# Another order of Strassen's seven products in the last gate of an encoder kernel

## The reference

```python
def _trunk(x, p, g_pre, g_post, w_ple, w_ple_gate, ...):
    for i in range(DEPTH):
        h = _rmsnorm(x, g_pre[i])
        ...
        x = x + _rmsnorm(o, g_post[i])
        x = x + jax.nn.sigmoid(x @ w_ple_gate[i]) * (p[i] @ w_ple[i])
    return x
```

## Time and profile before

| | us |
|---|---|
| median of three runs | 2026.52 |
| the profiled execution's own time | 2028.59 |
| its span, first to last instruction | 2026.8 |
| TensorE busy | 1929.4 |
| VectorE busy | 1174.0 |
| GpSimd busy | 781.5 |
| ScalarE busy | 689.6 |

### The profile page before, as it was taken

The page is one execution under the profiler, slowest core; times in us unless marked ns, Lnnn a source line. Parts: engine busy times, 40 slices in busy tenths (PEclk is TensorE's granted clock), DMA queues, the critical chain, the costliest instruction groups (busy, mean ns, idle before and its releaser), DMA issues. The chain is left out here.

```text
span 2026.8 us, 26398 instructions
## 1 busy us (share of the span) xinstructions
PE 1929.4 (95%) x9784; PEld 1607.2 (79%) x9784; DVE 1174.0 (58%) x1735; ACT 689.6 (34%) x1397; POOL 781.5 (39%) x552
## 2 busy tenths in 40 slices
PE   4999999999989999999999999999999999999699
PEld 3788888887889788788777888777989897887577
DVE  5599999736768227416743100365777773267675
ACT  6111212211668322112322111223777773323231
POOL 0110121122687444535433223213535362545473
PEclk9999999999989999999999999998999999999799
DMA  4202333443566646534211222583212225565424
GB/s 165 66 11 68 139 90 114 135 144 112 183 233 223 203 164 234 174 104 153 97 51 46 77 78 89 191 293 109 63 48 63 46 78 165 187 214 190 153 94 146
DMA packets 145185, 263.03 MB, mean 130 GB/s; under 512 B 30705, under 2 KB 69361, under 8 KB 144434
## 3 DMA queue, kind: packets, MB, share of 16 engines
q1 hardware_dynamic: 145074, 261.54, 39.4%
HBM read 173.22 MB, written 88.28 MB: 129 GB/s over the span
## 5 line engine op out<-in xcount | busy, mean ns | idle before, releaser
L589 DVE SCALAR_TENSOR_TENSOR ie_acc<-ie_u,ie_wconv,ie_acc 128x1551 f32<-128x1551 f32 x120 | 248.9, 2074 | 3.2
L187 POOL TENSOR_TENSOR w_lo_part<-w_raw,w_hi_part 128x1024 fp32r<-128x1024 f32 x24 | 67.3, 2804 | 333.7 <-ACT w_hi_part L179 333.7
L169 POOL TENSOR_TENSOR w_hi_part<-w_raw,zero 128x1024 fp32r<-128x1024 f32 x52 | 99.9, 1921 | 173.9 <-DMA w_raw<-wall 171.6
L1515 PE MATMUL op_ps<-w_hi_part,rows_hi 128*128 128x512 f32 x384 | 156.8, 408 | 5.1 <-DVE rows_lo L1153 2.6
L324 PE MATMUL ie_ps<-rows_hi,w_hi_part 128*128 128x512 f32 x384 | 152.4, 397 | 4.8 <-DVE w_lo_part L553 4.8
L324 PE MATMUL ie_ps<-rows_lo,w_hi_part 128*128 128x512 f32 x384 | 152.6, 397 | 0.0
L1515 PE MATMUL op_ps<-w_lo_part,rows_hi 128*128 128x512 f32 x384 | 152.2, 396 | 0.0
L1515 PE MATMUL op_ps<-w_hi_part,rows_lo 128*128 128x512 f32 x384 | 152.2, 396 | 0.0
L324 PE MATMUL ie_ps<-rows_hi,w_lo_part 128*128 128x512 f32 x384 | 150.9, 393 | 0.0
L171 POOL TENSOR_TENSOR w_lo_part<-w_raw,w_hi_part 128x1024 fp32r<-128x1024 f32 x52 | 130.1, 2503 | 4.1
L2851 DVE TENSOR_TENSOR mla_pt_lo<-mla_ps_t,mla_pt_hi 128x512 fp32r<-128x512 f32 x160 | 109.0, 686 | 26.2 <-ACT mla_pt_hi L2820 24.9
(11 more groups left out here) (289 smaller groups left out, 5184.1 us busy)
## 6 DMA issues: line engine op xcount, KB each, us to landing
w_raw<-wall SPq DMA_DIRECT2D x86, 512.0 KB, 4.8
op_in<-x SPq DMA_DIRECT2D x24, 512.0 KB, 4.5
x<-op_in SPq DMA_DIRECT2D x24, 512.0 KB, 3.0
pro_x<-x SPq DMA_DIRECT2D x12, 512.0 KB, 9.8
op_in<-attn SPq DMA_DIRECT2D x24, 256.0 KB, 2.9
o_half<-op_ost SPq DMA_DIRECT2D x24, 256.0 KB, 2.0
gt_p_raw<-p_fm SPq DMA_DIRECT2D x48, 128.0 KB, 3.3
op_orl<-o_half SPq DMA_DIRECT2D x24, 256.0 KB, 5.1
```

The lines of the kernel that those rows point to most:

```text
L169: pool.tensor_tensor(hi, raw, g.zero[:, 0:1].broadcast_to([P, QCOLS]), ALU.add).then_inc(g.w_hi, 1)
L589: dve.scalar_tensor_tensor(acc[:], ubuf[:, cc, s:s + CW], wconv[:, cc, s:s + 1], acc[:], ALU.mult, ALU.add).then_inc(taps, 1)
L1515: mm = pe.matmul(product_at(c * NT + t), g.XT[a][:, k, t * P:(t + 1) * P], w_at(g, name, m, k * HALF, HALF), start=k + a + m == 0, stop=k ...
```

## The change

The seven passes come in another order: A11, A12, S4, S2, S3, S1, A22. Output tiles are now finished in three passes: one a unit in A12, two a unit in S1, one a unit in A22; a third partial sum `Y` is held in the place of S4's rows. Three kinds of work change engine. The sums and low parts of the weights go from GpSimd to VectorE (`w_step`, 16 instructions of 1024 columns), except the sums for T1 and T4. The sum S1 of the rows goes from VectorE to GpSimd. The embeddings' high parts, from tile 2 on, go from GpSimd to ScalarE (`rows_high`); GpSimd keeps their low parts (`rows_low`). In the SyncE queue the embeddings are loaded before the residual rows, no longer after them, and only one weight block is loaded in the middle of the A12 pass, where one block and two quarters were. The diff, cut to its core:

```diff
                               self.g.XT[0][:, 2 * a:2 * a + 2, 0:HALF].bitcast(F32), ALU.subtract).then_inc(self.lo, 2)
 
 
-SEVEN = ("A11", "A12", "S2", "S3", "S1", "S4", "A22")
+SEVEN = ("A11", "A12", "S4", "S2", "S3", "S1", "A22")
...
     def sum_s2(self, dve, j):
-        dve.wait_ge(self.summed_k, 2 * j + 1)
-        dve.tensor_tensor(self.s2(j), self.row(1, 1, j), self.row(0, 0, j), ALU.subtract).then_inc(self.summed, 1)
+        dve.wait_ge(self.sums["S3"], j + 1)
+        dve.tensor_tensor(self.spare_at(j), self.row(1, 1, j), self.row(0, 0, j), ALU.subtract).then_inc(self.sums["S2"], 1)
 
     def sum_s4(self, dve, j):
         dve.wait_ge(self.lo, PAIRS_OF_TILES + j + 1)
-        dve.wait_ge(self.summed, 2 * j + 1)
-        dve.tensor_tensor(self.row(0, 1, j), self.row(0, 1, j), self.s2(j), ALU.subtract).then_inc(self.summed, 1)
+        dve.wait_ge(self.sums["S2"], j + 1)
+        dve.tensor_tensor(self.row(0, 1, j), self.row(0, 1, j), self.spare_at(j), ALU.subtract).then_inc(self.sums["S4"], 1)
+
+    def sum_s1(self, pool, j):
+        pool.wait_ge(self.sums["S3"], j + 1)
+        pool.tensor_tensor(self.row(1, 0, j), self.row(1, 0, j), self.row(1, 1, j), ALU.add).then_inc(self.sums["S1"], 1)
...
+        w_summed = {n: sem("sum_" + n) for n in ("T2", "T3", "T1", "T4")}
+        w_hi, w_lo = sem("w_hi"), sem("w_lo")
+
+        OUTPUTS = {1: [(0, 0)], 5: [(1, 1), (0, 1)], 6: [(1, 0)]}
+        UNITS = []
+        of_unit = [[] for _ in range(NU)]
+        for n in range(NU):
+            i, j = divmod(n, PAIRS_OF_TILES)
+            for half, c in OUTPUTS.get(i, []):
+                of_unit[n].append(len(UNITS))
+                UNITS.append((half * PAIRS_OF_TILES + j, c))
+        E = len(UNITS)
+        taken_by = [0]
+        for n in range(NU):
+            taken_by.append(taken_by[-1] + (n // PAIRS_OF_TILES in (2, 3, 4)))
+
+        SLOT = {"A11": (1, 0), "A12": (1, 1), "S4": (0, 0), "S2": (0, 1), "S3": (1, 0), "S1": (1, 1), "A22": (0, 0)}
+        BLOCK = {"B22": (0, 0), "T2": (0, 1), "T3": (1, 0), "T1": (1, 1), "T4": (0, 0)}
+        READY = ["B22", "T2", "T3", "T1", "T4"]
+        OF_PASS = {"S4": "B22", "S2": "T2", "S3": "T3", "S1": "T1", "A22": "T4"}
...
+            def load_embedding(e):
+                if e < 4:
+                    sp.wait_ge(ple.p_split, 2 * (e - 1))
+                else:
+                    sp.wait_ge(p_lo, e - 3)
+                sp.dma_start(ple.p_raw[:, e % 2], g.p_fm[l, UNITS[e][0]]).then_inc(ple.p_in[e % 2], 16)
...
-                    load_raw(B11, 1)
+                    load_block("T3", B22)
                 if n == 12:
...
+                for e in of_unit[n]:
+                    if e + 2 < E:
+                        load_embedding(e + 2)
+                for e in of_unit[n]:
+                    if e + 2 < E:
+                        load(e + 2)
+                    sp.wait_ge(x2_rows, 2 * (e + 1))
+                    t, c = UNITS[e]
+                    sp.dma_start(tiles_of(g.y, t)[:, c * HALF:(c + 1) * HALF], x2[:, e % 3]).then_inc(stored[e % 3], 16)
...
-            def low(name, q):
-                pool.wait_ge(w_hi, 2 * READY.index(name) + q + 1)
-                pool.tensor_tensor(quarter(name, q, 1), quarter(name, q), quarter(name, q, 0).bitcast(F32), ALU.subtract).then_inc(w_ready, 1)
...
-            ple.split_rows(pool, 2)
-            ple.split_rows(pool, 3)
-            low("T3", 0)
-            ple.split_rows(pool, 4)
-            low("T3", 1)
-            ple.split_rows(pool, 5)
+            def rows_low(e):
+                hi, lo = [x[:, e % 2] for x in ple.p]
+                pool.wait_ge(p_hi, e - 1)
+                pool.tensor_tensor(lo, ple.p_raw[:, e % 2], hi.bitcast(F32), ALU.subtract).then_inc(p_lo, 1)
+
+            for e in range(2, 6):
+                rows_low(e)
+            ple.split_weights(pool, 1)
...
+            rows_low(6)
+            rows_low(7)
+            for j in range(PAIRS_OF_TILES):
+                bl.sum_s1(pool, j)
...
-            W_HIGH = {4: ("T2", 0), 5: ("T2", 1), 6: ("T3", 0), 7: ("T3", 1), 14: ("T1", 0), 15: ("T1", 1),
-                      20: ("T4", 0), 21: ("T4", 1), 22: ("B22", 0), 23: ("B22", 1)}
+            W_HIGH = {5: ("B22", 0), 6: ("B22", 1), 11: ("T2", 0), 12: ("T2", 1), 15: ("T3", 0), 16: ("T3", 1),
+                      22: ("T1", 0), 23: ("T1", 1), 28: ("T4", 0), 29: ("T4", 1)}
...
+            def rows_high(e):
+                act.wait_ge(ple.p_in[e % 2], 16 * (e // 2 + 1))
+                act.wait_ge(ple.mm, e - 1)
+                act.copy(ple.p[0][:, e % 2], ple.p_raw[:, e % 2]).then_inc(p_hi, 1)
...
-                if whole(n) is not None:
-                    tanh(whole(n))
+                for e in of_unit[n]:
+                    tanh(e)
+                for e in of_unit[n]:
+                    if e + 2 < E:
+                        rows_high(e + 2)
...
+            W_STEPS = {6: ("T2", 0, 0), 7: ("T2", 0, 1), 8: ("T2", 1, 0), 9: ("T2", 1, 1), 10: ("B22", 2, 0), 11: ("B22", 2, 1),
+                       12: ("T3", 0, 0), 13: ("T3", 0, 1), 14: ("T2", 2, 0), 15: ("T2", 2, 1), 20: ("T3", 2, 0), 21: ("T3", 2, 1),
+                       26: ("T1", 2, 0), 27: ("T1", 2, 1), 32: ("T4", 2, 0), 33: ("T4", 2, 1)}
+
+            def w_step(name, step, q):
+                at = quarter(name, q)
+                if step == 0:
+                    dve.wait_ge(block_in[name], 16)
+                    dve.wait_ge(raw_in[q], 16)
+                    dve.tensor_tensor(at, at, g.raw[:, q], ALU.subtract).then_inc(w_summed[name], 1)
+                elif step == 1:
+                    dve.wait_ge(block_in["B22"], 16)
+                    dve.wait_ge(w_summed[name], q + 1)
+                    dve.tensor_tensor(at, at, quarter("B22", q), ALU.add).then_inc(w_summed[name], 1)
+                else:
+                    dve.wait_ge(w_hi, 2 * READY.index(name) + q + 1)
+                    if name == "T1":
+                        dve.wait_ge(w_summed["T4"], q + 1)
+                    dve.tensor_tensor(quarter(name, q, 1), at, quarter(name, q, 0).bitcast(F32), ALU.subtract).then_inc(w_lo, 1)
...
                 elif i == 5:
-                    dve.wait_ge(taken, 2 * PAIRS_OF_TILES + j + 1)
-                    total(e, u, product).then_inc(totalled, 1)
+                    dve.wait_ge(taken, taken_by[n - PAIRS_OF_TILES + 1])
+                    total(of_unit[n][0], v, product)
+                    total(of_unit[n][1], y, product)
                 else:
-                    total(e, v, product).then_inc(totalled, 1)
+                    total(of_unit[n][0], v, product)
...
             for n in range(NU + 1):
                 if n + AHEAD < NU:
                     bl.low(dve, n + AHEAD)
-                j = n - 4
                 if n < PAIRS_OF_TILES:
-                    bl.sum_k(dve, n)
-                if 0 <= j < PAIRS_OF_TILES:
-                    bl.sum_s2(dve, j)
+                    bl.sum_s3(dve, n)
+                if 0 <= n - 2 < PAIRS_OF_TILES:
+                    bl.sum_s4(dve, n - 2)
+                if n < PAIRS_OF_TILES:
+                    bl.sum_s2(dve, n)
+                if n in W_STEPS:
+                    w_step(*W_STEPS[n])
+                for e in of_unit[n - 1] if n else []:
+                    row(e)
                 if PAIRS_OF_TILES <= n < NU:
                     consume(n)
-                if 0 <= j < PAIRS_OF_TILES:
-                    bl.sum_s4(dve, j)
-                if n and whole(n - 1) is not None:
-                    row(whole(n - 1))
...
             def embedding(e):
-                c = COLS[e // PAIRS_OF_TILES]
+                c = UNITS[e][1]
                 if e == 0:
                     pe.wait_ge(bl.copied, NT)
-                pe.wait_ge(ple.p_split, 2 * (e + 1))
+                if e < 2:
+                    pe.wait_ge(ple.p_split, 2 * (e + 1))
+                else:
+                    pe.wait_ge(p_lo, e - 1)
+                    pe.wait_ge(x2_rows, 2 * (e - 2) + 1)
                 pe.wait_ge(ple.w_split, 2 * (c + 1))
-                if e >= 2:
-                    pe.wait_ge(x2_rows, 2 * (e - 2) + 1)
```

More of the change, by code:

```diff
@@ L1188, in source @@
         name = SEVEN[i]
-        return {"A11": self.row(0, 0, j), "A12": self.row(0, 1, j), "S2": self.s2(j), "S3": self.row(0, 0, j),
+        return {"A11": self.row(0, 0, j), "A12": self.row(0, 1, j), "S2": self.spare_at(j), "S3": self.row(0, 0, j),
                 "S1": self.row(1, 0, j), "S4": self.row(0, 1, j), "A22": self.row(1, 1, j)}[name]
@@ L1194, in wait_source @@
         name = SEVEN[i]
[L1195 to L1198, removed]
+        if name in self.sums:
+            eng.wait_ge(self.sums[name], j + 1)
         else:
@@ L1787, in gate_seven @@
         V = bl.spare_at
+        Y = lambda j: bl.row(0, 1, j)
         G = lambda e: bl.spare_at(PAIRS_OF_TILES + e % 2)
@@ L1793, in gate_seven @@
```

(21 more changed lines are left out.)

100 lines of the change are left out of this document (35 added, 65 removed).

## The result

The changed kernel takes 2034.25 us in the median of 7 runs (2029.59 to 2035.79); the kernel before, in 7 runs beside it, 2024.83 us (2022.59 to 2027.62). The ratio is 1.004, 95% interval 1.0028 to 1.0052: slower by some 9 us, where 1.0 was forecast. The profiled execution took 2034.25 us, its span is 2032.4, its mean granted clock 0.981.

A forecast was written before the change was run, and what follows sets the result against it. Waits in A12 through VectorE's row and GpSimd's low part bounded it beside TensorE's work. A12 gives 4.9 us, the rest costs 5.9: 1.0 more, median 2026.52 to 2027.5; range 2014 to 2037, forecast's own 2022.5 to 2032 (chance 0.50).

The forecast's parts named there:

- D: S1 pass: lower clock holds for whole units behind waits, TensorE becomes the bound; 9.2 us more, 2036.7; chance 0.10.
- E: A12 and S1 rounds meet GpSimd's low parts of embeddings, S2 and S3 fall behind; 8 more, 2035.5; chance 0.13.
- the two loads of an S1 round: S1, two tiles a unit: loads put at 2.8 us in a round of 7.9, or 9.1 with a T4 step.
- GpSimd in VectorE's way: End of A12: GpSimd's split of embeddings' weights delays the row's second instruction by 0 to 2.2 us, taken as 1.7.
- the lower clock behind A12: Lower clock counted at 1.5 us within product 12, nothing for the 17 products after it.
- Row of tile 0: Start of A12: first row instruction at 1870.8, so embedding(2) starts there and not at 1883.77; 12.9 us won.
- The round: A12 and S1: each row waits for a load the previous row set off; 7.3 us in A12 against TensorE's 4.2.
- S4, S2 and S3 without a wait: 17 products without an embedding: moved weight work costs nothing; passes at 50 us without a wait.
- S1: 43.9 forecast: S1 pass takes 43.9 us, 10.3 more than 33.6; against 4.4 lost before, the rest costs 5.9 more.
- A22 and the tail: A22: no high parts of rows left, 4.2 us a unit, loads awaited three rows later; costs nothing, tail the same.
- B: Shorter rounds: loads land 1.9 us after issue, seven rounds 0.9 shorter, no GpSimd meeting; 8 us less, 2019.5; chance 0.17.
- C: Round does not close: cast never late, only the block's load stops TensorE in A12, S1 loses nothing; 2006.6; chance 0.10.

The follow-up runs named there:

- Experiments 2: Changed kernel with ScalarE's cast of the embeddings one place later, behind the next high part of rows: 2007.28 us, ratio 0.9918 to the kernel before.
- 7: Changed kernel with the cast behind the next high part, plus the ten low parts of weights back on GpSimd: 2013.58 us, ratio 0.9945 to the kernel before.
- version 3: Changed kernel with SyncE loading tile e+4's embeddings ahead of its wait for row(e), embedding(3)'s ahead of the T3 block: 2014.07 us, ratio 0.9943.
- versions 9: Changed kernel with later cast and earlier embedding loads, plus B22's two low parts on GpSimd: 2010.41 us, ratio 0.9909 to the kernel before.
- 10: Changed kernel with later cast, earlier embedding loads and B22's low parts on GpSimd, plus ScalarE's next high part ahead of tanh: 1991.18 us, ratio 0.9828.
- 5: Changed kernel with the cast behind the next high part, plus embedding(3)'s load ahead of the T3 block: 2007.85 us, ratio 0.9923 to the kernel before.
- 6: Changed kernel with both the cast behind the next high part and embeddings loaded two tiles earlier: 2005.74 us, ratio 0.9908 to the kernel before.

## Why the prediction was wrong in size

The sign of its sum and its mechanism were right, and 2034.25 lies in the range. The forecast time was wrong: the loss is 9 us, not 1. The sign is partly luck: 1.0 was the difference of 5.9 and 4.9, with 2 us of play in the load alone, and "slower" had a chance of 0.31. The time also lies above the 2022.5 to 2032 given to the forecast itself; the range holds it because it made room for rivals D and E, and neither happened as described. What failed is the size of terms: the two loads of an S1 round, GpSimd in VectorE's way, and the lower clock behind A12, which was put at nothing. Times are counted from the gate's first low part on VectorE (1849.98 before, 1845.88 after), which is where the working started.

*Row of tile 0, and what A12 wins there: right.* embedding(2) was forecast 20.8 us after that point; it came at 21.3.

*The round: right as a mechanism, too short in S1.* I took 2.8 us for the load, near the lower end of 2.6 to 3.1. In A12 the loads of the chain took 3.43, 2.57 and 2.39 us and the one behind the block 5.95; in S1, where two loads are issued together, 3.27, 3.80, 3.72 and 3.86. So 2.8 was right for A12 (the mean of the three is 2.80) and 0.5 to 1.0 too short for S1; the one behind the block landed 1.2 later than forecast. Round for round: the one in A12 from 1878.9 to 1887.0 takes 8.1 against 7.3; 0.6 of the difference is the load, 0.2 the way from high part to step. The three in S1 take 9.9, 10.5 and 9.4 against 9.05, 9.05 and 7.9; the first of them by 0.5 of load and 0.3 of VectorE's low part of rows. I went below the median of before on the argument that the load's neighbours now come later. In S1 the neighbour is the other tile's load; that this is why the loads there are longer is not shown.

*GpSimd in VectorE's way: 1.7 taken, 3.1 measured.* GpSimd's two instructions ran from 1891.15 to 1896.8. They met two of VectorE's where I had reckoned with one: the step (2.91 instead of 1.21) and the row's second instruction (2.13 instead of 0.69):

```profile
1891.15 2.34 POOL L1264 TENSOR_TENSOR gt_w_ple_hi<-gt_w_ple_raw,zero 128x1024 fp32r<-128x1024 f32 x1
1893.57 3.22 POOL L1266 TENSOR_TENSOR gt_w_ple_lo<-gt_w_ple_raw,gt_w_ple_hi 128x1024 fp32r<-128x1024 f32 x1
```

The rule that the prediction took from the Trainium skill (SBUF — State Buffer, "Who interferes with whom") says that a VectorE instruction with two SBUF inputs and a GpSimd instruction that reads SBUF exclude each other. The trace agrees: the step began at 1891.66, 0.5 us after GpSimd's first instruction, and ended 1.1 us after that instruction's end, about its own length of 1.21 later. The first of the two on GpSimd, with a broadcast operand, blocked as well as the second. The prediction also read from the kernel before that VectorE's instructions in a row wait once together. That reading is wrong: there three in a row took 2.88, 2.83 and 2.82 us (from 1867.59 on), each held by itself.

*These together* put product 12's second half at 57.1 us where 53.8 was forecast, 3.3 too early: 1.4 by the round with the load behind the block, 0.8 by the next round, 1.4 by GpSimd, less 0.3 in the last part round. Product 12 ends at 59.9 where 56.7 was forecast. A12 should have given 4.9 us and gave 1.8.

*S4, S2 and S3 without a wait: right,* though nearer to the edge than I had costed. VectorE was busy for 46.63 of 49.90 us; the low parts of weights took 1.58 us in the mean and those of rows 1.22, not 1.2 and 0.6, since some of both lay beside GpSimd (up to 2.30). The stretch took 1.4 us more than 17 products at full clock; this is the granted 0.96 of its window and not a wait: behind product 12's wait the matmuls start 0.43 us apart until 1908.7. I had reckoned the lower clock in product 12 alone. Experiments 2 and 7 show that VectorE's weight work is not what costs.

*S1: 43.9 forecast, 48.4 measured.* Of the 4.5 us missing, 3.8 are the three rounds (0.8, 1.5 and 1.5, by their loads and by VectorE's low part of rows, which took 0.94, 1.07 and 1.16 us instead of 0.68 beside GpSimd's low parts of embeddings), 0.3 the first rows, which end later; the rest goes with the clock, 0.89 in that window, with TensorE's idle 9.4 us in it.

*A22 and the tail: right,* 29.3 us from its first product on, with no wait longer than 0.5; that is 0.3 shorter than before.

Sum: 3.1 + 1.4 + 4.5 - 0.3 = 8.7 us too little, with 1.0 forecast: 9.7, the difference in the gate's length.

The rivals: B (shorter rounds) went the wrong way: the loads behind the store took 2.4 to 3.9 us, not 1.9. C (the round does not close) is what the kernel does with the cast one place later, 2007.28 us where C said 2006.6: the round is closed by that one place. (C had S1 lose nothing, and 3.6 us of waits stayed there, so the close number is partly luck.) D's clock did not hold for whole units: 0.89 in S1 and not 0.5. E (VectorE) had the price by another way: the rounds do meet GpSimd's low parts of embeddings, but for 0.1 us in A12 and 0.3 to 0.5 in S1 instead of 0.7; the dear meeting is the one with the split of weights, and the falling behind in S2 and S3 is not there.

What I did not see at all is the second round (total, tanh, high part, low part), since the first hid it. One turn took 5.4 us in version 3, which is slow only against TensorE's 4.2 us, and it shows as soon as the first is open.

Open: how the 11.6 us between versions 9 and 10 divide. 1.2 us a unit in A12 were expected of it, and S1's waits of 1.6 went as well; I didn't separate them.

## What to carry to other kernels

An instruction that waits for a DMA belongs behind everything on its engine that others are waiting for. Whether it costs is decided by whether a ring closes: follow what is queued behind it until you come back to the transfer's own issue, add up the ring, and compare it with the bound engine's time for one turn (its starts, not the sum of its instructions' durations). For a ring taken several times, give each transfer the median, or more where transfers are issued in pairs: in S1 an error of 0.5 to 1.0 us was paid at every turn. And after a wait is removed, read the trace again before the gain is booked: in versions 3, 5 and 9 the next one, 0.9 to 2.9 us, stood right behind it.

## What the hardware showed that I had not expected

The same 128 KB load took 2.4 to 6.0 us from issue to landing in one profile between 1850 and 2000 us, with a median of 3.7. In the versions that issue it early (3, 6, 9, 10) the median in that window was 2.7, 2.6, 2.9 and 3.4, with 1.9 at the least and 10.0 at the most, so early issue alone doesn't settle it. The lower clock behind TensorE's waits is no small part of their cost: of the 9.7 us that the gate lost, 4.9 are idle and 4.8 are longer busy time, and the busy time of 165.3 us is 12.7 more than the same matmuls took at full clock in version 10. And a meeting of VectorE and GpSimd costs both: 3.2 us instead of 2.3 to 2.7 on GpSimd's side, up to 3.4 instead of 1.2 on VectorE's.
